# A three-part network kernel with the start, both ends of attention and the last norm put in another order

## What is computed

```python
def rms_norm(x, g):
    y = x * rsqrt(mean(x * x, axis=-1) + EPS)
    return y * g

# block 1 begins with
zxbcdt = rms_norm(x, ln_g) @ in_w            # in_w columns: z, xbc, dt

# block 2, attention: k, v from kv_ln_g, q from ln_g, both on the same x
k, v = split(rms_norm(x, kv_ln_g) @ kv_w);  k = rms_norm(k, k_norm_g)   # per head half
q = rms_norm(rms_norm(x, ln_g) @ q_w, q_norm_g)
lam = exp(sum(lv[0] * lv[1])) - exp(sum(lv[2] * lv[3])) + lam_init
# per head: two softmaxes over causal logits with a bias table
attn = p[:, :, 0] - lam * p[:, :, 1]
o = rms_norm(attn @ v, subln_g) * (1 - lam_init)
x = x + o.reshape(s, 1024) @ out_w
x = x + conv_ffn(x, ffn_ln_g[1], ...)
# the program ends with
x = x + merged @ w_out
return rms_norm(x, final_norm_g)
```

## Time and profile before

| | |
|---|---|
| median of 3 runs | 2252.2 us (2250.05 to 2257.27) |
| profiled execution | 2252.14 us, span 2250.3 us |
| TensorE busy | 2160.2 us, 96% |
| VectorE busy | 1400.6 us, 62% |
| ScalarE busy | 872.5 us, 39% |
| GpSimd busy | 37.2 us, 2% |
| mean granted TensorE clock | 0.982 of full |

### The profile page before, as it was taken

How to read it: one execution, slowest core, us unless ns; L and a number is a source line. 1 busy time by engine, 2 the same in 40 slices (tenths; PEclk the granted TensorE clock), 3 DMA queues, 4 the chain that set the end, 5 groups by cost and what they waited for, 6 DMA issues and landing times.

```text
span 2250.3 us, 26544 instructions
## 1 busy us (share of the span) xinstructions
PE 2160.2 (96%) x10196; PEld 1642.1 (73%) x10196; DVE 1400.6 (62%) x2038; ACT 872.5 (39%) x1451; POOL 37.2 (2%) x100
## 2 busy tenths in 40 slices
PE   8999989999999998998899999999999999999997
PEld 6777775468888886777678888787777777676445
DVE  6688886467776345566577776446767755555334
ACT  4465653134443233444254443234334322343302
POOL 0000000000000001111000000000000000000000
PEclk9999999999999999999999999999999999999998
DMA  4322211123322332111133232332222223111122
GB/s 161 110 66 66 66 57 57 56 85 99 97 93 89 91 108 87 62 59 39 38 101 96 93 102 86 91 109 86 75 66 75 76 74 124 45 47 43 51 85 75
DMA packets 54524, 179.41 MB, mean 80 GB/s; under 512 B 5999, under 2 KB 7151, under 8 KB 54168
## 3 DMA queue, kind: packets, MB, share of 16 engines
q1 hardware_dynamic: 51264, 167.79, 23.9%
q10 hardware_dynamic: 3160, 10.30, 1.4%
HBM read 175.95 MB, written 4.74 MB: 80 GB/s over the span
## 4 chain that ended last, share of the span: by engine, by line
PE 84%; DVE 11%; ACT 3%; issue 1%; DMA 1%; POOL 0%; DVEq 0%; ACTq 0%; POOLq 0%
PE bankpair L277 21%; PE bankpair L281 21%; PE bankpair L278 21%; PE bankpair L285 8%; DVE conv_rows L379 2%; DVE weights_low L312 1%; PE bankpair L1352 1%; ACT arena L2041 1%; PE bankpair L1385 1%; PE bankpair L668 1%; PE bankpair L1366 1%; PE bankpair L1206 1%; PE bankpair L1218 1%; PE bankpair L688 1%; DVE padded_rows L2097 1%
## 5 line engine op out<-in xcount | busy, mean ns | idle before, releaser
L277 PE MATMUL bankpair<-scaled_in_high,weights_high 128*128 128x512 f32 x1792 | 720.0, 402 | 3.8 <-DVE padded_rows L1594 2.2
L278 PE MATMUL bankpair<-scaled_in_low,weights_high 128*128 128x512 f32 x1792 | 700.4, 391 | 0.0
L281 PE MATMUL bankpair<-scaled_in_high,weights_low 128*128 128x512 f32 x1792 | 447.8, 389 | 0.0
L301 ACT ACTIVATE weights_high<-weight_ring 128x1024 fp32r<-128x1024 f32 (+3 forms) x312 | 303.7, 974 | 339.1 <-DMA weight_ring<-down_dram 155.3
L277 PEld LDWEIGHTS bankpair<-scaled_in_high,weights_high 128*128 128x128 f32 x1792 | 338.0, 189 | 82.8 <-DVE padded_rows L1594 6.4
L278 PEld LDWEIGHTS bankpair<-scaled_in_low,weights_high 128*128 128x128 f32 x1792 | 337.9, 189 | 73.7 <-issue 5.5
L281 PEld LDWEIGHTS bankpair<-scaled_in_high,weights_low 128*128 128x128 f32 x1792 | 336.6, 188 | 70.2
L312 DVE TENSOR_TENSOR weights_low<-weight_ring,weights_high 128x1024 fp32r<-128x1024 f32 (+3 forms) x312 | 349.0, 1128 | 60.0 <-ACT weights_high L301 51.4
L285 PE MATMUL bankpair<-arena,weight_ring 128*128 128x512 f32 x448 | 196.4, 599 | 3.3 <-DVE arena L2135 2.1
L285 PEld LDWEIGHTS bankpair<-arena,weight_ring 128*128 128x128 f32 x448 | 85.7, 193 | 109.9 <-issue 105.6
L278 PE MATMUL bankpair<-gated_low,weights_high 128*128 128x512 f32 x352 | 139.2, 396 | 0.0
(11 more groups left out here) (331 smaller groups left out, 2371.5 us busy)
## 6 DMA issues: line engine op xcount, KB each, us to landing
weight_ring<-up_dram SPq DMA_DIRECT2D x88, 512.0 KB, 3.4
weight_ring<-w_in_dram SPq DMA_DIRECT2D x70, 512.0 KB, 3.4
weight_ring<-in_w_dram SPq DMA_DIRECT2D x40, 512.0 KB, 3.5
weight_ring<-down_dram SPq DMA_DIRECT2D x32, 384.0 KB, 3.1
weight_ring<-kvq_dram SPq DMA_DIRECT2D x24, 512.0 KB, 3.4
weight_ring<-down_dram SPq DMA_DIRECT2D x32, 320.0 KB, 2.9
weight_ring<-out_a_dram SPq DMA_DIRECT2D x8, 512.0 KB, 3.4
weight_ring<-out_b_dram SPq DMA_DIRECT2D x8, 512.0 KB, 3.5
```

The costliest lines, as they stand in the source:

```text
L277: nc.tensor.matmul(bank, WH[:, high_slot, cell], high, start=(k == 0), stop=False)
L278: nc.tensor.matmul(bank, WH[:, high_slot, cell], low, start=False, stop=False)
L281: mm = nc.tensor.matmul(bank, WL[:, slot, cell], high, start=False, stop=(c == last_k))
L301: nc.scalar.activation(WH[:, (PART0[name] + k) % SLOTS, 0:n], RAW[:, b % SLOTS, 0:n], ACT.Copy).then_inc(high_ready, 1)
```

## The change

It puts work in another order and on another engine in five places; the mathematics stays.

- **Start.** ScalarE asks for the first 8 parameter columns alone, loads the table with the root at once, and asks for the rest of the parameters, the constants and the bias inputs after the seventh square. It makes the high halves of blocks 0, 2, 4 and 6. VectorE makes the others and all low halves, and one weight split before the last half instead of three. TensorE first makes nine products of ones with ones (128 x 128); then the cells of the dt tile follow the sums of squares one by one, three blocks behind, each cell with its low-weight product.
- **Entry to attention.** Lambda's sums are made before the first FFN, its last two steps after the low parts of the query. Three high and two low parts of the query instead of five and five lie before attention; the table with the root is loaded before them. The q tile of head 0 is read before k is scaled. Four cells of head 1 go ahead of the spreading of q's inverse, two behind it.
- **Heads 6 and 7.** `split_out` becomes `high_out` on ScalarE and `low_out` on VectorE, at other steps. The loop ends with head 7; what stood behind it is written out, with the cells of `attn_a` in smaller groups, and with the norms and halves of heads 6 and 7 ahead of the last reads.
- **Second FFN.** The sums of the last two squares go behind the first FFN tile; the table with the root is loaded ahead.
- **End.** The sums of squares are made as columns (products with a single column of ones, four position blocks), root and reciprocal are taken on 128 x 4, and four transposes spread them into bank 6.

```diff
-            spread_norm(0, 1)
-            for h in range(AH + 1):
+            for h in range(AH):
                 for i in range(NT):
                     w = NT * h + i
-                    quarter(*((h + 1, i + 1) if i < 3 else (h + 2, 0)))
-                    if h < AH:
-                        scores(h, i)
-                    if h >= AH - 1:
-                        out_fill(NT * (h - AH + 1) + i)
+                    if w == 0:
+                        cells_of(1, 6, 10)
+                        spread_norm(0, 1)
+                        cells_of(1, 10, 12)
+                    else:
+                        quarter(*((h + 1, i + 1) if i < 3 else (h + 2, 0)))
+                    scores(h, i)
+                    if h == AH - 1:
+                        out_cells(*OUT_FILL[i][0:2])
...
+            out_cells(24, 30)
+            turn_attn(AH - 1, 3)
+            attn_v(AH - 1, 2)
+            spread_out(AH - 2)
+            out_cells(30, 33)
+            attn_v(AH - 1, 3)
+            out_cells(33, 36)
+            out_sums(AH - 1)
+            out_cells(36, 42)
             spread_out(AH - 1)
...
+            def high_out(k):
+
+                act.wait_ge(gemm_done, TILE0["kvq"] + 3 * AH - 1)
+                act.wait_ge(oh_ready, k + 1)
+                nc.scalar.activation(HQH[:, k, :], OH[:, k, :], ACT.Copy).then_inc(oq_high, 1)
...
                     if i == 2 and h >= 1:
                         out_inverse(h - 1)
-                    if h >= AH - 1:
-                        split_high(act, BASE["attn_a"] + NT * (h - AH + 1) + i + 2)
+                    for k in HEADS_AT.get((h, i), ()):
+                        high_out(k)
...
+        HIGH_FIRST, LOW_FIRST = 3, 2
+        HEADS_AT = {(AH - 2, 2): (0, 1), (AH - 2, 3): (2, 3, 4), (AH - 1, 0): (5,)}
...
-            def split_out(k):
-
-                dve.wait_ge(gemm_done, TILE0["kvq"] + 3 * AH)
-                hq.step(nc.vector.tensor_copy(HQH[:, k, :], OH[:, k, :]))
-                hq.step(nc.vector.tensor_tensor(HQL[:, k, :], OH[:, k, :], HQH[:, k, :].bitcast(F32), ALU.subtract))
+            def low_out(k):
+
+                dve.wait_ge(oq_high, k + 1)
+                nc.vector.tensor_tensor(HQL[:, k, :], OH[:, k, :], HQH[:, k, :].bitcast(F32), ALU.subtract).then_inc(hq_ready, 2)
...
+            combine(AH - 1, 3)
+            split_low(dve, BASE["attn_a"] + 5)
+            add_part("attn_a", 3)
+            add_part("attn_a", 4)
+            split_low(dve, BASE["attn_a"] + 6)
+            out_norm(AH - 2)
+            low_out(AH - 2)
...
+            pe.wait_ge(acc_ready, acc_base(5) + KD)
+            for c in range(NT):
+                nc.tensor.matmul(BANK[7][:, c:c + 1], ACC[:, c * P:(c + 1) * P], ONES[:, 0:1], start=(c == 0), stop=False)
+            pe.wait_ge(sq_ready, KD * 6)
...
+            pe.wait_ge(last_inv, 1)
+            for c in range(NT):
+                mm = nc.tensor.transpose(BANK[6][:, c * P:(c + 1) * P], LASTI[:, c:c + 1].to_broadcast([P, P]), IDENT)
...
+            for _ in range(WARM):
+                nc.tensor.matmul(BANK[6][:, 0:P], ONES[:, :], ONES[:, :], start=True, stop=True)
```

228 lines of the change are left out of this document (152 added, 76 removed).

## The result

The changed kernel takes 2229.97 us (median of 5 runs, 2228.67 to 2236.43) against 2252.66 us (5 runs, 2250.05 to 2257.27): ratio 0.9903, 95% interval 0.9887 to 0.9919, some 23 us less. Forecast were 2224 and 28.4 us less, with 2219 to 2229 as the range of the main case and 2216 to 2233 as that of 8 in 10; the measured time lies 1 us above the first and inside the second. A second set gave 2229.46 us, ratio 0.9901 (0.9886 to 0.9916). The profiled execution of the first set was one of its longer ones: 2234.58 us, span 2232.8.

The account below looks back on a forecast made before the run. TensorE, busy 96% of the span, bounds the kernel, so only its waits and slow-clock time can be won. Gains 3.9 + 7.7 + 1.9 + 11.0 + 3.9 = 28.4 us give 2224 us, 8 in 10 within 2216 to 2233.

Parts of the forecast that it names:

- main case: Whole kernel: the five places' gains arrive about as summed, giving 2219 to 2229 us; chance 0.62.
- copies wait: Rival: ScalarE's copies hold up VectorE and TensorE at further heads, and its weight splits take 3 us: 2233; chance 0.15.
- the start gives nothing: Rival: TensorE bounds the start and its slow products eat the 3.9 us: 2228, inside the forecast's range, no separate chance.
- Start, forecast 3.9: Program start: high halves shared with ScalarE, first tile at 18.7 instead of 22.86 us, gain 3.9.
- Entry, forecast 7.7: Entry to attention: shorter wait for the key square 2.4, fewer slow products 1.5, covered second wait 3.8; from 5 to 9.
- The term for the clock: Entry to attention: half of the 2.6 us lost to slow products after the idle is won, 1.5, from 0 to 2.6.
- The rival that the clock stays up: Rival: no slow products after the entry's 2.5 idle, and head 7's copy early enough: 2217; chance 0.12.
- Head 7, forecast 1.9: Head 6 to head 7: the wait mostly moves from the scores to block (6, 2)'s turn; gain 1.9, or 7 without the copy wait.
- End of attention, forecast 11.0: End of attention: bank wait 2.5, low halves and slow products 5.0, last two sums behind the FFN tile 3.5; 6 to 12.
- Last norm, forecast 3.9: Program end: column sums and small root and reciprocal cut last square to output row from 6.2 to 2.2 us, gain 3.9.
- It moves as a block: Rest of the program: order kept, no transfer tied to a fixed time, so earlier gains reach the end whole.
- The slower case: Rival: the lower clock is granted in the alternating start and stays over the first input tiles: 2260; chance 0.03.

Follow-up runs that it names:

- best: Changed kernel with heads 0 to 3's subtractions behind head 7's query scaling and the first key tile's square ahead of two high parts: 2221.2 us, ratio 0.9859.
- second profile: Changed kernel run and profiled again, nothing edited: 2229.46 us, profiled span 2224.2.
- shifted kernels: Kernel before with two or four extra array clearings on VectorE ahead of the first half, delaying the program: 2258.0 us (ratio 1.0015) and 2259.99 us (1.0016).

## Why the prediction was right, and where it was not

The direction and the places held; the likeliest time was 6 us too low. The measured time lies inside the range of 8 in 10, but 1 us outside the 2219 to 2229 of the main case (0.5 in the second set), between it and the rival *copies wait* (2233) and near *the start gives nothing* (2228). That the main case and not a rival came true is read from the stretches, not from the time. The sum of the five was to be 24 to 33 and is (24.8 and 28.1). The other sign of being wrong, a wait in the unchanged stages that grows, did show: 3.61 to 4.66 at the `cmp_w` transfer in the first profile.

**Start, forecast 3.9, measured 3.65 to 4.0 with the ones.** The mechanism is as told: TensorE is the bound from the fourth sum on, one sum and three products per 1.55 us, no wait for VectorE. The landing of the first data was put at 4.2, and the first square started at 4.86. The estimate went by the bytes moved, which made even the first input piece 0.5 too early (4.67); what came last, at 4.84, was the smallest transfer, 8 columns of parameters issued at 0.74. 18.7 plus 0.66 is 19.4 against 19.22 measured.

**Entry, forecast 7.7, measured 6.4 to 9.7.** The wait for the square fell by 2.7 (forecast 2.4), the second wait went whole. The term for the clock, "half" of 2.6, is not a size but a case: of the seven profiles that keep its order, two with a long drop behind the first wait gave 6.4 and 6.6, two with a shorter one 8.0 and 8.1, and three without one 9.5 to 9.7. The rival that the clock stays up came true here in those three.

**Head 7, forecast 1.9, measured 1.5 five times and -0.2 twice.** The wait moved as forecast, 4.8 at the turn against 4.4. The step that failed is the walk from there to the scores: they were put 2.9 behind the turn and came 4.4 behind it, because the turn, the value products and the spreading (1.06 us for four, 0.60 at full pace) ran at the lower clock behind the longer wait. In the two profiles with -0.2 the query's first products were slow as well (0.43 us apart in place of 0.23). That the copy was the cause, and that without it 7 would be had, is borne out in kind: 5.15 in *best*.

**End of attention, forecast 11.0, measured 10.7 to 11.05** in all profiles that keep the order; the two sums 3.5 against 3.7 to 3.8. Right in each part.

**Last norm, forecast 3.9, measured 3.8 to 3.9.** From the last square to the first output row it is 2.4 (forecast 2.2), where it was 6.2.

**"It moves as a block" is the step that failed.** The terms themselves were nearly whole: 28.1 in the second profile against 28.4. But what lies between them gave back 1.5 to 8 us, though no instruction of TensorE in it had moved and its long waits had the same length but for one (the `cmp_w` transfer: 3.6 before, 3.4 to 4.7 now; "no transfer in it is tied to a fixed time" left out that the transfer itself takes longer in one execution than in another). At the forecast's places the clock was priced, elsewhere it was taken as fixed. The shifted kernels and the grid of the clock's changes show that the drops belong to the moment: a program whose parts lie otherwise against the grid meets another set of them, and the kernel before was lucky at 1550 in both its profiles. Of the losses, the one of 1.6 at 1525 is shown so; that the others (1700, 1890 to 1910, 2090 in the first profile) are of the same kind is read from their clock, and 1.05 of the first profile's is the transfer.

**The rivals.** Copies became a new wait of weight only in (6, 2); VectorE waited for a copy in four more places, which cost TensorE 1.1 in all, under the 6 of the rival. The start gave its 3.9, so it did not give nothing. The slower case wanted a low clock in the alternating start, and the granted clock was 1.00 in all of it.

## What to carry to other kernels

Sum the terms at the places of change, but expect a change of timing to redraw the clock drops everywhere else, by a few us either way; look for that before looking for a cause, by profiling the same program twice and the old one with a small delay at its start. Two profiles that match can do so by chance. Where an engine takes over a copy from another, ask what stands behind the *consumer* of the copy in its queue: two subtractions of 0.7 us placed one step too early took more than half of what was to be had there (1.5 left, 3.8 one step later). A norm's scale that only multiplies rows at the end is cheaper as a few columns: 3.8 us here, most of it the reciprocal, 3.35 us on 512 elements per partition and 0.18 on 4.

## What the runs showed of the hardware

- TensorE's clock fell after 2.2 us of waiting in 11 of 14 profiles and stayed up in 3, at the same instruction. In the first profile of the changed kernel it also fell where TensorE never waited, behind two pairs of product records with only 4 rows (records grow from 0.39 to 0.63); in the second the same four records, at 1696.99, were followed by no drop:

```profile
1699.95 1.12 PE L1260 MATMUL bankpair<-arena,constants 4*128 4x512 f32 x2
1700.92 1.02 PE L1261 MATMUL bankpair<-arena,constants 4*128 4x512 f32 x2
...
1703.49 0.63 PE L284 MATMUL bankpair<-scaled_in_high,weights_high 128*128 128x512 f32 x1
```

- At the very start the sums took 5.3 and 6.6 us for eight records without the ones, and 4.86 with them (twice), while the windows give the granted clock as 1.00 there. The trace has no record of the clock before its first change, the rise at 8.51 and 11.39 us; so in the first microseconds the column is not to be trusted, and the durations are.
- A transfer of 128 rows of 32 bytes took 4.1 us from issue (0.74) to the instruction that waited for it (4.86), as the list of transfers has it too. The 512 KB of the first input piece, asked for at the same time, landed at 4.67, only 0.17 earlier than the 4 KB.
